# mLSTM stage of a hybrid decoder step: four heads written out as one pipeline, decay rows spread by DMA, decays on GpSimd, norm on ScalarE

## The reference, cut to what matters

```python
def mlstm_chunk(carry, inp):
    c, n, m = carry
    q, k, v, li, lf = inp
    bcum = jnp.cumsum(lf, axis=1)
    d = bcum[:, :, None, :] - bcum[:, None, :, :] + li[:, None, :, :]
    d = jnp.where(causal[None, :, :, None], d, -jnp.inf)
    inter = bcum + m[:, None, :]
    m_row = jnp.maximum(inter, jnp.max(d, axis=2))
    w_intra = jnp.exp(d - m_row[:, :, None, :])
    w_inter = jnp.exp(inter - m_row)
    s = jnp.einsum('bthd,bshd->btsh', q, k) * w_intra
    num = jnp.einsum('btsh,bshv->bthv', s, v) + w_inter[..., None] * jnp.einsum('bthd,bhdv->bthv', q, c)
    den = jnp.sum(s, axis=2) + w_inter * jnp.einsum('bthd,bhd->bth', q, n)
    h = num / jnp.maximum(jnp.abs(den), jnp.exp(-m_row))[..., None]
    ...
    c_new = dec[..., None, None] * c + jnp.einsum('bsh,bshd,bshv->bhdv', w_end, k, v)
```

## Time and profile before

| | us |
|---|---|
| median of three runs | 4004.59 (4000.39 to 4005.97) |
| the profiled execution | 4008.49 |
| its span in the profile | 4006.7 |
| mLSTM stage, from SyncE's first load to the last product | 207.1 |

### The profile page before, as it was taken

The page is one execution under the profiler, slowest core; times in us unless marked ns, Lnnn a source line. Parts: engine busy times, 40 slices in busy tenths (PEclk is TensorE's granted clock), DMA queues, the critical chain, the costliest instruction groups (busy, mean ns, idle before and its releaser), DMA issues. The chain is left out here.

```text
span 4006.7 us, 53892 instructions
## 1 busy us (share of the span) xinstructions
PE 3608.9 (90%) x20016; PEld 3159.5 (79%) x20016; DVE 1738.4 (43%) x3292; ACT 1111.9 (28%) x2008; POOL 412.5 (10%) x1060
## 2 busy tenths in 40 slices
PE   5999667998998878999999997989889899999997
PEld 4999564545555567999999996988559799999997
DVE  5444313454454434434334346424662543343446
ACT  2434222333433334211111124202223411111113
POOL 0000103444443400000000000000000000000000
PEclk9999787989999978999999998999779899999998
DMA  4222442121211112111111101222321111111111
GB/s 119 95 94 94 150 140 67 33 66 35 60 41 24 30 32 77 43 42 37 48 41 47 42 26 39 94 72 88 126 73 43 42 38 47 42 47 42 42 42 50
DMA packets 306624, 241.65 MB, mean 60 GB/s; under 512 B 76322, under 2 KB 271206, under 8 KB 306490
## 3 DMA queue, kind: packets, MB, share of 16 engines
q1 hardware_dynamic: 294794, 197.03, 16.8%
q0 software_dynamic: 11696, 42.87, 2.9%
HBM read 181.27 MB, written 58.59 MB: 60 GB/s over the span
## 5 line engine op out<-in xcount | busy, mean ns | idle before, releaser
L451 PE MATMUL ffn_ps<-ffn_in_hi,ffn_w_hi 128*128 128x368 f32 x2112 | 703.9, 333 | 34.2 <-DVE ffn_w_lo L894 22.0
L452 PE MATMUL ffn_ps<-ffn_in_lo,ffn_w_hi 128*128 128x368 f32 x2112 | 702.1, 332 | 0.0
L453 PE MATMUL ffn_ps<-ffn_in_hi,ffn_w_lo 128*128 128x368 f32 x2112 | 700.3, 332 | 0.0
L451 PEld LDWEIGHTS ffn_ps<-ffn_in_hi,ffn_w_hi 128*128 128x128 f32 x2112 | 400.3, 190 | 40.7 <-DVE ffn_w_lo L894 23.1
L452 PEld LDWEIGHTS ffn_ps<-ffn_in_lo,ffn_w_hi 128*128 128x128 f32 x2112 | 400.2, 189 | 0.5
L453 PEld LDWEIGHTS ffn_ps<-ffn_in_hi,ffn_w_lo 128*128 128x128 f32 x2112 | 400.4, 190 | 0.0
L451 PE MATMUL ffn_ps<-ffn_h_hi,ffn_w_hi 128*128 128x368 f32 x1056 | 353.6, 335 | 10.7 <-DVE mix L967 9.8
L453 PE MATMUL ffn_ps<-ffn_h_hi,ffn_w_lo 128*128 128x368 f32 x1056 | 349.0, 330 | 0.0
L452 PE MATMUL ffn_ps<-ffn_h_lo,ffn_w_hi 128*128 128x368 f32 x1056 | 348.2, 330 | 0.0
L967 DVE TENSOR_TENSOR mix<-ffn_ps,mix 128x368 f32<-128x368 f32 x480 | 255.7, 539 | 191.5 <-PE ffn_ps L453 190.8
L838 ACT ACTIVATE ffn_w_hi<-ffn_w_raw 128x1024 fp32r<-128x1024 f32 x132 | 136.1, 1046 | 463.1 <-PE ffn_ps L453 463.1
(11 more groups left out here) (487 smaller groups left out, 6653.3 us busy)
## 6 DMA issues: line engine op xcount, KB each, us to landing
ffn_w_raw<-in_w_ffn_gate_dram SPq DMA_DIRECT2D x44, 512.0 KB, 3.9
ffn_w_raw<-in_w_ffn_up_dram SPq DMA_DIRECT2D x44, 512.0 KB, 3.9
ffn_w_raw<-in_w_ffn_down_dram SPq DMA_DIRECT2D x44, 512.0 KB, 3.6
ab_w_raw<-in_w_in_ab_dram SPq DMA_DIRECT2D x27, 512.0 KB, 3.9
...
```

Source lines behind the costliest of these rows:

```text
L451: pe.matmul(out, w_hi, x_hi, start=first, stop=False)
L452: pe.matmul(out, w_hi, x_lo, start=False, stop=False)
L453: return pe.matmul(out, w_lo, x_hi, start=False, stop=last)
```

## The change

- The two gate stages' results go to DRAM: `project_og_and_gates` stores `rows` and `ends` (`rows_d`, `ends_d`), and `mlstm` loads each head's two rows spread over all 128 partitions (`row_b`), and `ends` once (`dec`). The spread matmuls and their selector go.
- GpSimd makes the exponents `e` and the queries `q_int` (`decays`, seven operations a head): those of heads 0 and 1 at once, those of head i+2 after head i's states are stored.
- `qk_act`, `row_b`, `q_int`, `e`, `cx` and `cs` are there twice, for even and odd heads; `h` has a second place for tile 0.
- The heads are written out, and one list `order` runs through all four. New kinds: `exp` (ScalarE's exponentials of the next head, after tile 7), `root` (Ln and Exp of a group of tiles on ScalarE, a product `shift` on VectorE, then the normalisation on ScalarE by an Identity activation with scale and bias), `turn` (one half of one group: TensorE's transposes into the one bank `B_TURN`, VectorE's products into `mix`). Four of a head's six turns come in tiles 0 to 3 of the next head.

```diff
+            sp.wait_ge(end_exp, 2)
+            part_waits(sp, parted)
+            sp.dma_start(rows_d, rows[:, :, :]).then_inc(gates_stored, 16)
+            sp.dma_start(ends_d, ends[:, :]).then_inc(gates_stored, 16)
             sp.wait_ge(edge_stored, 32)
-            sp.wait_ge(gates_stored, 32)
+            sp.wait_ge(gates_stored, 64)
...
+    turns = [(g, x) for g in range(len(GROUPS)) for x in range(2)]
+    order = []
+    for i in range(HC):
+        order += [("start", i)] + ([("exp", 0)] if i == 0 else []) + [("prep", i, 0)]
+        for n in range(N):
+            order += ([("prep", i, n + 1)] if n + 1 < N else []) + [("main", i, n)]
+            if i and n < 4:
+                order += [("turn", i - 1) + turns[2 + n]]
+            if n == 6:
+                order += [("root", i, 0)]
+            if n == 7 and i + 1 < HC:
+                order += [("exp", i + 1)]
+            if n >= 8:
+                order += [("turn", i) + turns[n - 8]]
+        order += [("root", i, 1), ("root", i, 2), ("end", i)]
+    order += [("turn", HC - 1) + turn for turn in turns[2:]]
...
+        qk_act, q_int = s.sb("qk_act", [P, 2, 2, T]), s.sb("q_int", [P, 2, T])
+        row_b, dec = s.sb("row_b", [P, 2, 2, T]), s.sb("dec", [P, HC, N_ENDS])
...
+        e, st = s.sb("e", [P, 2, N, P]), s.sb("st", [P, 2, P])
...
+        h_all = s.sb("h", [P, N + 1, DV])
+        cx, cs = s.sb("cx", [P, 2, VX]), s.sb("cs", [P, 2, NSEQ, VX])
...
+            def load_rows(i):
+                for x in range(2):
+                    sp.dma_start(row_b[:, i % 2, x, :], rows_d[i, x:x + 1, :].to_broadcast([P, T])
+                                 ).then_inc(rows_in[i % 2], 16)
...
+            load_rows(0)
+            load_qk(0)
+            load_two(v, vd, 0, v_in)
+            sp.dma_start(dec[:, :, :].rearrange("p h n -> p (h n)"),
+                         ends_d.rearrange("(o h) n -> o (h n)", o=1).to_broadcast([P, HC * N_ENDS])).then_inc(once_in, 16)
...
+            load_state(0)
+            load_qk(1)
+            load_rows(1)
             load_two(gate, og, 0, og_in)
...
+            for i in range(HC - 1):
+                sp.wait_ge(pe_done, PE(f"{i}.s{SAMPLE}"))
                 part_waits(sp, parted)
-                load_qk(i + 1)
                 load_two(v, vd, i + 1, v_in)
-                sp.wait_ge(saved, i + 2)
-                part_waits(sp, parted)
-                load_state(i + 1)
-                sp.wait_ge(dve_done, DVE.before(i + 1))
+                if i + 2 < HC:
+                    sp.wait_ge(pool_done, POOL_OPS * (i + 1))
+                    part_waits(sp, parted)
+                    sp.wait_ge(dve_done, DVE(f"{i}.q_seq"))
+                    part_waits(sp, parted)
+                    load_qk(i + 2)
+                    load_rows(i + 2)
+                    sp.wait_ge(saved, i + 1)
+                    part_waits(sp, parted)
+                    load_state(i + 2)
+                sp.wait_ge(dve_done, out_done(i, *turns[-1]))
                 part_waits(sp, parted)
                 load_two(gate, og, i + 1, og_in)
 
...
+            def decays(i):
+
+                at = i % 2
+                pool.wait_ge(rows_in[at], (i // 2 + 1) * 32)
+                if i >= 2:
+                    pool.wait_ge(dve_done, DVE(f"{i - 2}.s{SAMPLE}"))
+                parts = [(P, slice(1, SAMPLE), full, masks), (N_META, slice(0, 1), col_of[0], masks),
+                         (TS, slice(SAMPLE, N), col_of[SAMPLE], s_mask)]
+                for k, (L, tiles, tokens, mask) in enumerate(parts):
+                    x = e[0:L, at, tiles, 0:L]
+                    shape = [L, tiles.stop - tiles.start, L]
+                    pool.tensor_tensor(x, row_b[0:L, at, 0, tokens].rearrange("p (n t) -> p n t", t=L),
+                                       cols[0:L, 0, tiles, i:i + 1].to_broadcast(shape), ALU.subtract).then_inc(pool_done, 1)
+                for k, (L, tiles, tokens, mask) in enumerate(parts):
+                    x = e[0:L, at, tiles, 0:L]
+                    shape = [L, tiles.stop - tiles.start, L]
+                    pool.wait_ge(pool_done, POOL_OPS * i + k + 1)
+                    pool.tensor_tensor(x, x, mask[0:L, 0:L].unsqueeze(1).to_broadcast(shape), ALU.add).then_inc(pool_done, 1)
+                pool.wait_ge(x_in[at], (i // 2 + 1) * 32)
+                if i >= 2:
+                    pool.wait_ge(pe_done, PE(f"{i - 2}.o{LAST}"))
+                pool.tensor_tensor(q_int[:, at, :], qk_act[:, at, 0, :], row_b[:, at, 1, :], ALU.mult).then_inc(pool_done, 1)
...
 
-            with pool.Fori(0, HC - 1) as i:
+            decays(0)
+            decays(1)
+            for i in range(HC):
                 store_states(i)
-            store_states(HC - 1)
+                if i + 2 < HC:
...
+                if n == 0:
+                    part_waits(pe, parted)
+                    pe.wait_ge(pool_done, POOL_OPS * (i + 1))
...
+            def turn(i, g, x):
+                last = before(i, g, x)
+                if last:
+                    pe.wait_ge(dve_done, out_done(*last))
+                pe.wait_ge(act_done, ACTS(f"{i}.hn{GROUPS[g][-1]}"))
+                part_waits(pe, parted)
+                for k, n in enumerate(GROUPS[g]):
+                    L = rows_of[n]
+                    mm = pe.transpose(ps[:, B_TURN, k * P:k * P + L], h_of(i, n)[0:L, x * P:x * P + P],
+                                      c["ident"][0:L, 0:L])
+                mm.then_inc(pe_done, 1)
...
+            def exponentials(i):
+                at = i % 2
+                act.wait_ge(pool_done, POOL_OPS * i + POOL_OPS - 1)
+                step(act.activation(e[0:N_META, at, 0, 0:N_META], e[0:N_META, at, 0, 0:N_META], ACT.Exp, scale=-1.0))
+                step(act.activation(e[0:TS, at, SAMPLE, 0:TS], e[0:TS, at, SAMPLE, 0:TS], ACT.Exp, scale=-1.0))
+                step(act.activation(e[:, at, 1:SAMPLE, :], e[:, at, 1:SAMPLE, :], ACT.Exp, scale=-1.0))
...
+            def root(i, g):
+                tiles = GROUPS[g]
+                L = rows_of[tiles[-1]]
+                at = slice(tiles[0], tiles[-1] + 1, tiles[1] - tiles[0])
+                act.wait_ge(dve_done, DVE(f"{i}.stat{tiles[-1]}.1"))
+                step(act.activation(rstd[0:L, at].unsqueeze(2), mv[0:L, at, 1:2], ACT.Ln, bias=eps[0:L, :]))
+                act.wait_ge(act_done, ACTS(f"{i}.log{g}"))
+                step(act.activation(rstd[0:L, at], rstd[0:L, at], ACT.Exp, scale=-0.5))
+                act.wait_ge(dve_done, DVE(f"{i}.shift{g}"))
+                act.wait_ge(act_done, ACTS(f"{i}.root{g}"))
+                for n in tiles:
+                    r = rows_of[n]
+                    step(act.activation(h_of(i, n)[0:r, :], h_of(i, n)[0:r, :], ACT.Identity, scale=rstd[0:r, n:n + 1],
+                                        bias=shift[0:r, n:n + 1]))
...
+                dve.wait_ge(act_done, ACTS(f"{i}.root{g}"))
+                step(dve.scalar_tensor_tensor(out=shift[0:L, at].unsqueeze(2), in0=mv[0:L, at, 0:1], scalar=-1.0,
+                                              in1=rstd[0:L, at].unsqueeze(2), op0=ALU.mult, op1=ALU.mult))
```

410 lines of the change are left out of this document (210 added, 200 removed).

## The result

The change is faster: 3974.94 us (median of 4 runs, 3967.34 to 3977.91) beside 4004.43 (4 runs, 4000.39 to 4005.97), ratio 0.9925, 95% interval 0.9908 to 0.9942. The forecast was 3973.

What follows compares the result with a forecast made beforehand. In the mLSTM stage's tiles TensorE and VectorE were taken as close to full, with head fronts and tails to overlap: 13.1 + 31.9 + 3 x (6.5 + 34.0) + 9.3 = 175.8 us against 207.1, giving 3973 us; range 3955 to 3990.

Steps and rivals of the forecast that it cites:

- The mechanism: mLSTM stage: heads overlap, about 40 us from one head's first main matmul to the next, GpSimd's 8.3 us a head covered.
- B: Tiles: interleaving doesn't overlap, TensorE and VectorE wait for each other, a head 4 us longer, 3989 us; chance 0.14.
- E: Whole kernel: no difference, GpSimd and VectorE blocking each other together with interleaving that doesn't overlap, 4004 us; chance 0.04.
- Start: Stage start to first main matmul: row loads 4.5 us, then GpSimd's chain 8.3, main at about 13.1; bounds 12 and 18.
- the loads' bound of 12: Stage start: low bound, 12 us, when dec and nw land behind the rows, qk and v.
- The norm inside the head: Before main 8: ScalarE's norm delays it 2.2 us, with the next head's exponentials 2.8 a head; bounds 0 and 4.
- Identity operations above 0.5 us: ScalarE's normalisation: a listed sign that the prediction is wrong; it took 0.4 us for each operation.
- The boundary: From a head's last update matmul's end (U) to the next head's first main matmul (M): 6.5 us; bounds 4.5 and 9.
- Heads 1 to 3: First main matmul to end of last update: 34.0 us each, against 29.1 before, with half clock in the first tiles.
- The end: After the last head's last update: four turns share one bank, each waiting for a product, 9.3 us against 9.9 before.
- Rival C: Tiles: GpSimd and VectorE block each other, two thirds of 8.3 us a head, 4 x 5.5 = 22 us, 3995; chance 0.06.
- Rival D: Next head's decays come late from GpSimd; saving gone above 3.4 times 8.3 us, at four times 4020 us; chance 0.04.

Runs made afterwards that it cites:

- run 1: Kernel before the change with only its loop over the heads written out, so waits are on constants: 4001.84 us beside 4004.73, stage 206.6.
- run 6: Changed kernel with the next head's start, exponentials and first two preps ordered ahead of this head's last norm groups, piece before main 8 left: 3952.21 us, stage 159.9.
- run 2: Changed kernel with 22 matmuls whose result nobody reads behind the two preps at each head boundary: 3966.9 us, stage 171.1.
- Run 8: Changed kernel with nine more GpSimd products of 128 x 1104 in front of q_int in heads 2 and 3: 3980.57 us, stage 191.4.
- run 9: Changed kernel with GpSimd's decays waiting for the previous head's last update and exponentials at their own head's start: 4001.31 us, stage 201.8.
- run 10: Changed kernel with the next head started ahead of the last norm groups, first group's norm spread, normalisation on VectorE: 3957.72 us, ratio 0.9887, stage 164.4.
- run 11: Run 10 with GpSimd's decays of heads 2 and 3 waiting for VectorE's last normalisation of the head before: 3944.20 us, ratio 0.9857, stage 151.2.

## Why the prediction was right, and where it was off

- *The mechanism* was right. A head and its boundary were to cost 40.5 us and cost 41.1 (before 50.9): TensorE waits at each boundary for ScalarE's kw, the clock is at 0.50 behind it and near 1.00 some 8 us on, there is a gap before main 8, and GpSimd works 7.6 us a head (8.3 in the prediction) and is never waited for after the start. Rivals B (a stage of 192) and E (207) fall with the stage at 182.0, and run 1 takes away the reading that the unrolling did it.
- *The stage was to be 175.8 us and was 182.0.* The 6.2 us lie in four terms: start 1.6, head 0 1.2, boundaries 3 x 0.7, end 1.8, less 0.5 in heads 1 to 3. The forecast for the whole still hit within 2 us, because code before the stage, untouched, ran 4.5 us shorter in the profiled execution, which came out at 3977.9 for the 3977.2 in the sum. That part was luck.
- *Start, 13.1 against 14.7.* The sum has GpSimd's chain last. Its parts were off both ways: the rows took 6.5 us to land, not 4.5 (I had counted them alone at the queue's rate, but qk and v were issued 0.9 and 2.0 us behind and shared it), and the seven operations took 7.6 us, not 8.3 (in the kernel before, VectorE's thirteen for the same values add up to 4.7), so the query product was there at 14.2. But TensorE did not wait for it. It waited for v, whose second half landed at 12.3, and then ran the preps of tiles 0 and 1 without a gap, at a granted clock of 0.50, up to the first main:

```profile
2803.88 0.58 PE L3471 MATMUL mlstm_ps<-ident,mlstm_v 128*16 128x128 f32 x2 [18.20 <-DMA mlstm_v<-qkv_proj]
...
2805.47 0.63 PE L3479 MATMUL mlstm_ps<-mlstm_qk_act 128*128 128x128 f32 x2
2806.03 1.03 PE L3495 MATMUL mlstm_ps<-mlstm_vx,mlstm_st 16*16 16x257 f32 x2
```

  The two preps behind v, 2.2 us, are what the loads' bound of 12 left out. The port is held here too: VectorE's copy of the n row took 0.99 us (0.10 in later heads) and ended with GpSimd's q_int, at 2805.58, and st of tile 0 came behind it, done at 2805.65. That cost nothing, because TensorE was in the preps until then.
- *The norm inside the head, 2.2 us of gap.* Measured 2.40. The Identity operation came out at 0.59 us, four in 2.07, where I took 0.4 a piece from its neighbours; "Identity operations above 0.5 us" was one of my signs of error, and it applied. In head 0 I had left out that the clock, at 1.00 until there, falls in that gap: 0.89 and 0.68 in the two stretches of 4 us from 2824, as in run 6. That goes with its 33.1 for 31.9.
- *The boundary, 6.5 against 7.2.* The same term: the six Identity operations took 3.0 us (2882.79 to 2884.77 and 2885.51 to 2886.51), where my steps have 2.3. The rest of the chain came within 0.2 us of what I wrote (Ln at U + 1.2, the first Identity at U + 2.6, M 0.8 us behind the last).
- *Heads 1 to 3, 34.0 against 33.9.* Right as a sum, less so in its parts: the clock cost 3.7 us (run 2), not 2.6, and waits without registers gave back 0.6 inside a head (run 1), which I had at nothing.
- *The end, 9.3 against 11.1.* Four turns through one bank: TensorE waits 4.18 us for ScalarE's last Identity and then 1.02, 1.01 and 0.68 for VectorE's products. I had named the mechanism and priced it too low.
- *Rival C* was priced as a share of GpSimd's time and given 0.06. In the changed kernel it does not happen in the tiles (cx takes 0.48 us as in the kernel before, beside GpSimd or not). But it is there as an all-or-nothing wait, and the change escapes it by the order alone: GpSimd's work falls on the first tiles (2845.6 to 2853.2), the shifts and the q_seq copy elsewhere. Runs 8 and 9 put them together and their stages are 9 and 20 us longer than the change's, of which the held shift by itself is 3 and 16; run 10's is 13 us longer than run 11's.
- *Rival D*, decays late, was not reached, and was not tested to its end. In the changed kernel GpSimd begins 6.5 us behind U and is done at U + 14.0 (9 and 17.5 in the prediction); head 2's exponents were complete at 2850.7 and ScalarE took them up at 2870.1, 19 us later. Run 8's extra products stand behind the six operations that the exponentials wait for, so they delay the query product alone, which was still 13.9 us ahead of the next M. It shows that four times the usual GpSimd work has room before TensorE waits for it, not how late the exponents may come.

Not tried: a shorter start (it would have to bring forward both v and GpSimd's chain, which end within 0.5 us of each other as seen from the first main), and two banks for the last turns.
